# Reordering the start of a conv / attention / mixture-of-experts trunk, and moving its output bias to GpSimd

## The chip, the cores and the metric

The kernel runs on one core of one Trainium2 chip. The metric is the device time of one execution in microseconds; the kernel before takes 1702.82 us (median of 3 runs, 1698.28 to 1706.78). The core has five engines with instruction queues of their own: TensorE (PE; its weight loads are listed as PEld), VectorE (DVE), ScalarE (ACT), GpSimd (POOL) and SyncE (SP), which issues most transfers. The engines meet at semaphores. The transfers themselves run on 16 DMA engines of the core.

## The reference

Two residual layers over 512 tokens of width 1024, float32. Layer 0 mixes tokens with a Conformer convolution module, layer 1 with differential attention. After each comes a mixture of 32 gated experts, two for each token. The part that the change touches is the first mixer:

```python
def conformer_conv(h, w_in, b_in, dw, dw_b, ln_g, ln_b, w_out, b_out):
    u = h @ w_in + b_in                      # 1024 -> 2048
    a, g = jnp.split(u, 2, axis=-1)
    u = a * jax.nn.sigmoid(g)
    u = causal_depthwise_conv(u, dw) + dw_b  # 31 taps, each channel by itself
    u = jax.nn.silu(layer_norm(u, ln_g, ln_b))
    return u @ w_out + b_out
...
h = rms_norm(x, norm1_g[0])
x = x + conformer_conv(h, ...)               # this is where b_out comes in
h = rms_norm(x, norm2_g[0])
x = x + hierarchical_moe(h, ...)
```

## The kernel before, in words

All five engines run a hand-written program; nothing reorders it. Tokens lie in 4 tiles of 128, channels in 8 blocks of 128 (`ct`).

**Transfers.** SP issues them in program order (from L401): the four tiles of x (512 KB each, into `x_res`) with one small gain vector, then weight units 0 and 1 of `conv_w_in`, then the parameters of the convolution, then units 2 and 3, two units of `conv_w_out`, and 24 small ones. A weight unit is 2 MB, issued as two halves of 1 MB by `load_unit` (L315) into one of the six slots of `ring`. The parameters are six transfers that count on one semaphore, `params_loaded`: `conv_dw`, 31 rows of 4 KB (L408), three single rows of 4 KB (L410), the two rows of `conv_b_in` (L411), and the row of `conv_b_out` (L412). They go to `area3`, one parameter row per partition.

**Start.** For each token tile ACT takes the squares (L618), DVE inverts the root (L814), ACT scales the tile into `xn` (L624, semaphore `xn_done`), PE transposes it (L1158) and DVE writes it to `hT` (L820). PE then waits for all six parameter transfers, transposes the parameter rows in 8 small transposes into PSUM bank 5 (L1179), and DVE copies the result to `chan`, one column per parameter (L835), and signals `chan_taken` (L836). PE waits for that and for units 0 and 1, and begins the products.

**Products and convolution.** For each block `ct`, PE computes the two halves of the gated unit with 8 matmuls of 128x512 each (`project`, L1170) and signals `glu_ready`. ACT makes the gate (`gate`, L639), DVE the product (`gated`, L843, which needs `chan`). The 31 taps of a block are split: ACT multiplies 12 of them (L652) and POOL adds these up (L515), DVE does the other 19 (L860, L863), and then adds POOL's sum (L871, L872). Halfway through the taps of block ct, ACT makes the gate of block ct + 1, and stops there until PE has it. From ct = 3 on PE also sums the columns of finished blocks for the layer norm (`stats`, L1185, L1186), into banks 4 and 5.

**Output of the mixer.** `mix_out` (L1206) forms 8 results of 128 tokens by 512 columns. Each is 8 matmuls (L1221) and then one matmul of a row of ones with a half of the bias row (L1224), which adds `b_out`. DVE adds each result to `x_res` (`add_mix`, L892). In the second half PE puts the transposes of the next norm and the router's logits (L1158, L1240) between the results. Routing, the gather of rows by POOL (L525), and the expert loop follow (L1263 to L1290), each step released by the one before.

Of the kernel before, what the change touches and what calls it, by code (L numbers as in the profile page):

```python
# [27 lines left out]
ALU = mybir.AluOpType  # L28
# [3 lines left out]
P = 128  # L32
D = 1024
T = 512
NT = T // P
NC = D // P
EPS = 1e-6
TAPS = 31
# [27 lines left out]
def trunk(nc, x, norm1_g, norm2_g, conv_w_in, conv_b_in, conv_dw, conv_dw_b, conv_ln_g, conv_ln_b,  # L66
# [5 lines left out]
    def sb(name, shape, dt=F32):  # L72
        return ctx.enter_context(nc.sbuf_tensor(name, shape, dt))

    def sem(name):
        return ctx.enter_context(nc.semaphore(name))

    with ctx:

        x_res = sb("x_res", [P, NT, D])  # L80
# [3 lines left out]
        area2 = sb("area2", [P, UNIT])  # L84
        area3 = sb("area3", [P, UNIT])
        scratch = sb("scratch", [P, 5632])
        ident = sb("ident", [P, P])
        ones = sb("ones", [P, P])
# [29 lines left out]
        bank = [banks2[i // 2][:, i % 2, :] for i in range(8)]  # L118
# [10 lines left out]
        consts_ready, params_loaded, x_loaded = sem("consts_ready"), sem("params_loaded"), [sem(f"x_loaded{t}") for t in range(NT)]  # L129
# [6 lines left out]
        ssq_done, std_done, xn_done = sem("ssq_done"), sem("std_done"), sem("xn_done")  # L136
# [4 lines left out]
        chan_ready, chan_taken = sem("chan_ready"), sem("chan_taken")  # L141
        glu_ready, gate_done, u_done = sem("glu_ready"), sem("gate_done"), sem("u_done")
        tap_made, tap_added, conv_done, sq_done = sem("tap_made"), sem("tap_added"), sem("conv_done"), sem("sq_done")
        stats_ready, ln_var, ln_std, ln_x, ln_done = sem("stats_ready"), sem("ln_var"), sem("ln_std"), sem("ln_x"), sem("ln_done")
        mix_ready, mix_taken = sem("mix_ready"), sem("mix_taken")

        xn_stored, logits_ready, exp_in, exp_done = sem("xn_stored"), sem("logits_ready"), sem("exp_in"), sem("exp_done")
# [42 lines left out]
        def cols_dram(w, c0, width=512):  # L190

            v = w[:, c0:c0 + width].rearrange("(h p j) n -> h p j n", h=2, j=4)
            return [v[h] for h in range(2)]
# [12 lines left out]
        sq_ct = area1[:].rearrange("p (c t) -> p c t", c=NC)  # L206
        uT = area2[:].rearrange("p (c t) -> p c t", c=NC)
        chan_rows = area3[0:TAPS + 5, 0:D]
        b_out = area3[0:1, 3072:3072 + D]
        PAD = TAPS - 1  # L210
        u_buf = [scratch[:, b * (T + PAD):(b + 1) * (T + PAD)] for b in range(2)]
        base = 2 * (T + PAD)
# [52 lines left out]
        oT = area2[:].rearrange("p (h t) -> p h t", h=HEADS)  # L265
# [45 lines left out]
        def _(sp):  # L311
# [11 lines left out]
            def mix_unit(n, src):  # L323

                load_unit(chunk_halves(unit(n)), src, unit_loaded[n % RING])
# [74 lines left out]
            w_in, w_out = conv_w_in[0], conv_w_out[0]  # L400
            for t in range(NT):  # L401
                sp.dma_start(x_res[:, t, :], x[0, t * P:(t + 1) * P, :]).then_inc(x_loaded[t], 16)
                if t == 0:
                    sp.dma_start(norm_g[:, 0, :], norm1_g[0].rearrange("(h p j) -> p h j", h=2, j=4)).then_inc(gain_loaded, 16)
            mix_unit(0, cols_dram(w_in, 0))
            mix_unit(1, cols_dram(w_in, D))

            sp.dma_start(chan_rows[0:TAPS, :], conv_dw[0]).then_inc(params_loaded, 16)  # L408
            for r, vec in enumerate((conv_dw_b, conv_ln_g, conv_ln_b)):
                sp.dma_start(chan_rows[TAPS + r:TAPS + r + 1, :], vec).then_inc(params_loaded, 16)  # L410
            sp.dma_start(chan_rows[TAPS + 3:TAPS + 5, :], conv_b_in[0].rearrange("(r n) -> r n", r=2)).then_inc(params_loaded, 16)  # L411
            sp.dma_start(b_out, conv_b_out).then_inc(params_loaded, 16)  # L412
            mix_unit(2, cols_dram(w_in, 512))
            mix_unit(3, cols_dram(w_in, D + 512))
            for n in range(2):
# [18 lines left out]
            n0 = FIRST[1]  # L434
# [35 lines left out]
        def _(pool):  # L470
            g = nc.gpsimd
# [32 lines left out]
                                 pattern=[[1, P]], channel_multiplier=-1))  # L504
            g.memset(step_count[:], 0.0).then_inc(consts_ready, 1)


            k = 0
            for ct in range(NC):
# [292 lines left out]
        def _(dve):  # L802
# [44 lines left out]
            for ct in range(NC):  # L847
                ub = u_buf[ct % 2]
                dve.wait_ge(u_done, ct + 1)

                k0 = tap_count[0]
                for k, w in enumerate(range(POOL_TAPS, TAPS)):
                    acc = sums[k % 2]
                    dst = uT[:, ct, :] if w == TAPS - 1 else acc
                    if k >= 2:
                        dve.wait_ge(dve_taps, k0 + k - 1)
                    elif ct >= 1:
                        dve.wait_ge(conv_done, ct)
                    if k < 2:
                        ins = v.tensor_scalar(acc, ub[:, w:w + T], chan[:, ct, w:w + 1],  # L860
                                              chan[:, ct, TAPS:TAPS + 1] if k == 0 else 0.0, ALU.mult, ALU.add)
                    else:
                        ins = v.scalar_tensor_tensor(dst, ub[:, w:w + T], chan[:, ct, w:w + 1], acc, ALU.mult, ALU.add)  # L863
                    ins.then_inc(dve_taps, 1)
                tap_count[0] += TAPS - POOL_TAPS
                if ct + 1 < NC:
                    gated(ct + 1)
                dve.wait_ge(dve_taps, tap_count[0])
                dve.wait_ge(tap_added, (ct + 1) * (POOL_TAPS - 1))
                last = sums[(TAPS - POOL_TAPS) % 2]  # L870
                link(v.tensor_tensor(last, pacc[ct % 2], last, ALU.add))  # L871
                v.tensor_tensor(uT[:, ct, :], uT[:, ct, :], last, ALU.add).then_inc(conv_done, 1)  # L872
# [10 lines left out]
                v.tensor_tensor(uT[:, ct, :], uT[:, ct, :], ln_r, ALU.mult).then_inc(ln_x, 1)  # L883

            def add_mix(l):

                for n in range(2):
                    for t in range(NT):
                        k = NT * n + t
                        dve.wait_ge(mix_ready, 8 * l + k + 1)  # L890
                        xs = x_res[:, t, n * 512:(n + 1) * 512]
                        ins = v.tensor_tensor(xs, xs, mix_bank(l, k)[:], ALU.add)  # L892
                        if n == 0:
                            ins.then_inc(mix_taken, 1)
                        else:
                            ins.then_inc(x_done, 1)
                            invert_rms(N_MOE[l], t)
                            if t >= 1:
                                take_hT(N_MOE[l], t - 1)
                take_hT(N_MOE[l], NT - 1)  # L900
# [108 lines left out]
            for l in range(LAYERS):  # L1009
                n = N_MOE[l]  # L1010
# [137 lines left out]
        def _(pe):  # L1148
            mm = nc.tensor.matmul
# [23 lines left out]
            pe.wait_ge(consts_ready, 1)  # L1173
            for t in range(NT):
                transpose_xn(N_PRE[0], t)
            pe.wait_ge(params_loaded, 16 * 6)
            R = TAPS + 5
            for ct in range(NC):
                last = nc.tensor.transpose(bank[5][:, ct * R:(ct + 1) * R], chan_rows[:, ct * P:(ct + 1) * P], ident[0:R, 0:R])  # L1179
            last.then_inc(chan_ready, 1)  # L1180


            def stats(ct):
                pe.wait_ge(sq_done, ct + 1)
                mm(bank[4][:], ones[:], uT[:, ct, :], start=ct == 0, stop=ct == NC - 1)  # L1185
                return mm(bank[5][:], ones[:], sq_ct[:, ct, :], start=ct == 0, stop=ct == NC - 1)  # L1186

            pe.wait_ge(xt_taken, 8)
            pe.wait_ge(chan_taken, 1)
            for ct in range(NC):  # L1190
                ua, ug = (0, 1) if ct < 4 else (2, 3)
                loaded(pe, ua)
                loaded(pe, ug)
                if ct >= 2:
                    pe.wait_ge(u_done, ct - 1)
                cols = slice((ct % 4) * P, (ct % 4 + 1) * P)
                project(bank[2 * (ct % 2)][:], w_chunks(ua), hT, cols)
                last = project(bank[2 * (ct % 2) + 1][:], w_chunks(ug), hT, cols)
                last.then_inc(glu_ready, 1)
                if ct >= 3:  # L1200
                    stats(ct - 3)
            stats(NC - 3)
            stats(NC - 2)
            stats(NC - 1).then_inc(stats_ready, 1)

            def mix_out(l, n0, src, bias):  # L1206


                for n in range(2):
                    loaded(pe, n0 + n)  # L1210
                for n in range(2):
                    for t in range(NT):
                        k = NT * n + t
                        dst = mix_bank(l, k)
                        if n == 1:
                            pe.wait_ge(mix_taken, NT * l + t + 1)
                        for c in range(NC - 1 if k < ahead[l] else 0, NC):
                            if k == 0:

                                pe.wait_ge((ln_done, oT_done)[l], c + 1)  # L1220
                            last = mm(dst[:], src[:, c, t * P:(t + 1) * P], w_chunks(n0 + n)[:, c, :],  # L1221
                                      start=c == 0, stop=c == NC - 1 and not bias)
                        if bias:
                            last = mm(dst[:], ones[0:1, :], b_out[:, n * 512:(n + 1) * 512], start=False, stop=True)  # L1224
                        last.then_inc(mix_ready, 1)
                        if n == 1 and t >= 1:
                            transpose_xn(N_MOE[l], t - 1)
                        if n == 1 and t >= 2:
                            logits(l, t - 2)
                transpose_xn(N_MOE[l], NT - 1)  # L1230
                logits(l, NT - 2)
                logits(l, NT - 1)
# [126 lines left out]
                        pe.wait_ge(over_w2[l], j * 32 + 32)  # L1359
                        down(o, 0, unit(n1 + 2), j + 1).then_inc(o["y_ready"], 1)  # L1360

            mix_out(0, 4, uT, True)
            route(0)
            pe.wait_ge(lists_done, 1)
            experts(0)
# [4 lines left out]
            n0 = FIRST[1]  # L1370
# [106 lines left out]
            for h, g, e in attention_steps():  # L1477
# [51 lines left out]
                    output_T(e)  # L1529
                if h is not None:  # L1530
                    v_half(h, 1)
            mix_out(1, n0 + 6, oT, False)
            route(1)
            pe.wait_ge(lists_done, 2)
            experts(1)
# [22 lines left out]
```

## Time and profile before

| | us |
|---|---|
| median of 3 runs (lowest to highest) | 1702.82 (1698.28 to 1706.78) |
| the profiled execution, whole | 1700.86 |
| its span | 1699.1 |
| PE busy | 1408.8 (83%) |
| DVE busy | 440.7 (26%) |
| ACT busy | 328.0 (19%) |
| POOL busy | 277.2 (16%) |

The span covers the instructions of the program; 1.8 us of the execution lie around it. A matmul on float32 appears as two MATMUL instructions. Of the chain that ended last, 49% of the span is PE and 33% DMA, the latter nearly all the weights of the experts. The part that the change touches lies in the first 270 us: start to 31.5 us, products and convolution to 187 us, layer norm to 205 us, output of the mixer to 269 us. The granted TensorE clock is told in shares of full speed, 2.4 GHz; 0.5 is its lower level, 1.2 GHz.

### The profile page before, as it was taken

How to read it: one execution, taken by the hardware profiler on the slowest of the kernel's cores; microseconds unless marked ns; L12 is line 12 of the kernel's file. 1: busy time of each engine (PE TensorE's matmuls, PEld its weight loads, DVE VectorE, ACT ScalarE, POOL GpSimd, SP SyncE). 2: the span in 40 equal slices, each digit the busy share in tenths (PEclk: the TensorE clock that was granted, in tenths of full speed). 3: DMA queues.
4: the chain of work that ended last, by engine and by line, in shares of the span. 5: the costliest groups of instructions: out<-in, count | busy, mean ns of one | idle time of the engine just before them, and what ended most of it. 6: DMA issues, size and time to landing. Idle time of an engine off the chain costs nothing.

```text
span 1699.1 us, 17050 instructions
## 1 busy us (share of the span) xinstructions
PE 1408.8 (83%) x6028; PEld 638.2 (38%) x6028; DVE 440.7 (26%) x858; ACT 328.0 (19%) x629; POOL 277.2 (16%) x381
## 2 busy tenths in 40 slices
PE   4996596898878788777599999996997888888784
PEld 2442144333223223232376676644332332233231
DVE  1699615111011111010333333325110110110112
ACT  2465311000000000000334434421010000000000
POOL 0688200211111111110000000000211111111110
PEclk9998697999999999898799999997998999999997
DMA  9122015789999999998600400315899999999994
GB/s 324 37 99 99 1 74 222 318 361 419 420 420 420 420 421 418 419 416 339 248 1 1 149 1 1 149 74 223 338 360 420 421 420 420 420 416 413 418 413 184
DMA packets 91249, 473.13 MB, mean 278 GB/s; under 512 B 19675, under 2 KB 19675, under 8 KB 40260
## 3 DMA queue, kind: packets, MB, share of 16 engines
q1 hardware_dynamic: 78500, 443.12, 64.3%
q0 software_dynamic: 10400, 16.82, 2.7%
q10 hardware_dynamic: 2304, 12.58, 1.9%
q8 instruction: 29, 0.48, 0.1%
q14 instruction: 16, 0.13, 0.0%
HBM read 466.43 MB, written 23.33 MB: 288 GB/s over the span
## 4 chain that ended last, share of the span: by engine, by line
PE 49%; DMA 33%; DVE 7%; POOL 4%; issue 3%; SPq 3%; ACT 1%; ACTq 0%; POOLq 0%; DVEq 0%
DMA ring<-in_moe_w 30%; PE banks L1273 19%; PE banks L1381 7%; PE banks L1221 5%; POOL scratch L515 4%; PE banks L1290 3%; PE banks L1414 3%; SPq L315 2%; PE banks L1170 2%; DVE banks L863 2%; PE banks L1473 1%; PE banks L1428 1%; PE banks L1455 1%; DMA area<-y_dram 1%; PE banks L1402 1%
## 5 line engine op out<-in xcount | busy, mean ns | idle before, releaser
L1273 PE MATMUL banks<-ring,scratch 128*64 128x512 f32 x1984 | 502.2, 657 | 143.8 <-DMA ring<-in_moe_w 131.3
L1273 PEld LDWEIGHTS banks<-ring,scratch 128*64 128x64 f32 x1984 | 157.9, 151 | 484.8 <-issue 484.8
L1006 DVE COPY scratch<-banks 128x256 f32<-128x256 f32 x65 | 27.6, 424 | 801.7 <-PE banks L1281 801.7
L1290 PE MATMUL banks<-ring,scratch 128*64 128x512 f32 x1008 | 231.8, 602 | 3.0 <-DVE scratch L1006 3.0
L680 ACT ACTIVATE scratch<-banks 64x512 f32<-64x512 f32 x65 | 38.2, 588 | 598.8 <-PE banks L1273 598.8
L533 POOL COPY at_out<-rows_out 128x1 int32 (+1 forms) x64 | 11.6, 181 | 705.2 <-ACT scratch L684 705.2
L515 POOL TENSOR_TENSOR scratch<-scratch 128x512 f32<-128x512 f32 x88 | 111.8, 1271 | 63.6 <-ACT scratch L652 51.6
L1381 PE MATMUL banks<-hT,ring 128*128 128x512 f32 x256 | 117.9, 604 | 0.8 <-DVE hT L820 0.8
L1170 PE MATMUL banks<-hT,ring 128*128 128x512 f32 x256 | 113.2, 603 | 0.7 <-issue 0.7
L1290 PEld LDWEIGHTS banks<-ring,scratch 128*64 128x64 f32 x1008 | 68.3, 137 | 118.7 <-issue 111.7
L1221 PE MATMUL banks<-ring,area 128*128 128x512 f32 x200 | 91.3, 609 | 10.6 <-ACT area L662 9.6
L684 ACT ACTIVATE scratch<-banks 128x512 f32<-128x512 f32 x65 | 38.8, 597 | 286.0 <-PE banks L1290 286.0
L863 DVE SCALAR_TENSOR_TENSOR banks<-scratch,chan,banks 128x512 f32<-128x512 f32 x128 | 85.0, 748 | 0.0
L525 POOL DMA_INDIRECT scratch<-xn_dram,at_in x64 | 67.1, 1048 | 56.2 <-POOL at_in L522 53.9
L652 ACT ACTIVATE scratch<-scratch,chan 128x512 f32<-128x512 f32 x96 | 66.7, 718 | 49.0 <-POOL scratch L515 35.2
L536 POOL DMA_INDIRECT y_dram<-scratch,at_out x64 | 65.6, 1025 | 56.5 <-POOL at_out L533 56.5
L543 POOL MEMSET scratch<- 128x512 f32 x4 | 2.1, 524 | 437.1 <-DVE x_res L892 437.0
L1170 PEld LDWEIGHTS banks<-hT,ring 128*128 128x128 f32 x256 | 49.5, 194 | 63.0 <-issue 63.0
L1381 PEld LDWEIGHTS banks<-hT,ring 128*128 128x128 f32 x256 | 46.2, 190 | 49.5 <-issue 46.9
L1414 PE MATMUL banks<-ring,hT 128*128 128x128 f32 x512 | 60.4, 276 | 0.0
L1221 PEld LDWEIGHTS banks<-ring,area 128*128 128x128 f32 x200 | 37.6, 194 | 60.7 <-issue 55.6
L1414 PEld LDWEIGHTS banks<-ring,hT 128*128 128x128 f32 x512 | 58.4, 192 | 0.0
(205 smaller groups left out, 1144.6 us busy)
## 6 DMA issues: line engine op xcount, KB each, us to landing
ring<-in_moe_w SPq DMA_DIRECT2D x374, 1024.0 KB, 16.9
area<-in_moe_w SPq DMA_DIRECT2D x12, 1024.0 KB, 10.2
ring<-in_attn_w_qkv SPq DMA_DIRECT2D x12, 1024.0 KB, 14.6
ring<-in_conv_w_in SPq DMA_DIRECT2D x8, 1024.0 KB, 14.4
area<-y_dram ACTq DMA_DIRECT2D x8, 1024.0 KB, 7.9
ring<-in_conv_w_out SPq DMA_DIRECT2D x4, 1024.0 KB, 12.5
xn_dram<-area ACTq DMA_DIRECT2D x8, 512.0 KB, 2.7
hT<-in_moe_w SPq DMA_DIRECT2D x4, 1024.0 KB, 7.6
```

What stands on the lines that cost most here:

```text
L515: g.tensor_tensor(pacc[ct % 2], pacc[ct % 2], tap[(k - 1) % TAP_BUFS], ALU.add).then_inc(tap_added, 1)
L525: g.indirect_dma_start(out=xe[s], out_offset=None, in_=xn_dram[l][:, :], in_offset=bass.IndirectOffsetOnAxis(ap=at_in[:, s:s + 1], axis=0) ...
L536: g.indirect_dma_start(out=y_dram[l][:, :], out_offset=bass.IndirectOffsetOnAxis(ap=at_out[:, s:s + 1], axis=0), in_=y_sb[s], in_offset=No ...
L652: a.activation(dst, u_buf[ct % 2][:, w:w + T], ACT.Copy, scale=chan[:, ct, w:w + 1]).then_inc(tap_made, 1)
L684: a.activation(y_sb[s], bank[6 + s][:], ACT.Copy).then_inc(sems["y_taken"], 1)
L863: ins = v.scalar_tensor_tensor(dst, ub[:, w:w + T], chan[:, ct, w:w + 1], acc, ALU.mult, ALU.add)
L1170: last = mm(dst, w[:, c, cols], src[:, c, :], start=start and c == 0, stop=stop and c == NC - 1)
L1221: last = mm(dst[:], src[:, c, t * P:(t + 1) * P], w_chunks(n0 + n)[:, c, :], start=c == 0, stop=c == NC - 1 and not bias)
L1273: last = mm(bank[2 + s][q * SLOTS:(q + 1) * SLOTS, :], xeT[s][:, j, h, :], w[:, c, :], start=c == 0, stop=c == NC - 1)
L1290: last = mm(bank[6 + s][q * SLOTS:(q + 1) * SLOTS, :], hidT[s][:, j, :], w2c[:, j, q * 512:(q + 1) * 512], start=j == 0, stop=j == 3)
L1381: last = mm(qk_bank[c][:], w_chunks(u)[:, k, (h % 4) * P:(h % 4 + 1) * P], hT[:, k, :], start=k == 0, stop=k == NC - 1)
L1414: last = mm(v_bank[:, t * P:(t + 1) * P], hT[:, k, t * P:(t + 1) * P], w_chunks(u)[:, k, (h % 4) * P:(h % 4 + 1) * P], start=k == 0, stop= ...
```

## The change

It does four things.

1. SP issues the parameter transfers right behind x and in front of units 0 and 1. `conv_b_out` is no longer a row among them: it is loaded as 128 equal rows into `b_wide`, in the first quarter of `area2`, 512 KB in all, with a semaphore of its own, `bias_loaded`. `params_loaded` now counts five transfers.
2. PE does the products of block 0 first and the 8 parameter transposes behind them (`columns`). Its wait for `chan_taken` moves from ahead of all products to ct = 3, ahead of the first `stats`, which writes the bank that the transposes used.
3. The 8 bias results of `mix_out` go.
4. POOL adds `b_wide` to `x_res` tile by tile once ACT has read the tile for `xn`, in 4 additions of 128x1024, behind its constants and ahead of the taps. DVE waits for `bias_added` at the last two taps of block 0 (`area2`, where `b_wide` lies, is where the finished block is written) and ahead of `add_mix(0)`.

```diff
@@ sp
-            mix_unit(0, cols_dram(w_in, 0))
-            mix_unit(1, cols_dram(w_in, D))
-
             sp.dma_start(chan_rows[0:TAPS, :], conv_dw[0]).then_inc(params_loaded, 16)
             for r, vec in enumerate((conv_dw_b, conv_ln_g, conv_ln_b)):
                 sp.dma_start(chan_rows[TAPS + r:TAPS + r + 1, :], vec).then_inc(params_loaded, 16)
             sp.dma_start(chan_rows[TAPS + 3:TAPS + 5, :], conv_b_in[0].rearrange("(r n) -> r n", r=2)).then_inc(params_loaded, 16)
-            sp.dma_start(b_out, conv_b_out).then_inc(params_loaded, 16)
+            sp.dma_start(b_wide, conv_b_out.to_broadcast([P, D])).then_inc(bias_loaded, 16)
+            mix_unit(0, cols_dram(w_in, 0))
+            mix_unit(1, cols_dram(w_in, D))
             mix_unit(2, cols_dram(w_in, 512))
@@ pool
+            pool.wait_ge(bias_loaded, 16)
+            for t in range(NT):
+                pool.wait_ge(xn_done, t + 1)
+                g.tensor_tensor(x_res[:, t, :], x_res[:, t, :], b_wide, ALU.add).then_inc(bias_added, 1)
@@ dve, in the taps of a block
+                    if ct == 0 and w >= TAPS - 2:
+                        dve.wait_ge(bias_added, NT)
@@ dve, add_mix
+                if l == 0:
+                    dve.wait_ge(bias_added, NT)
@@ pe
-            pe.wait_ge(params_loaded, 16 * 6)
-            R = TAPS + 5
-            for ct in range(NC):
-                last = nc.tensor.transpose(bank[5][:, ct * R:(ct + 1) * R], chan_rows[:, ct * P:(ct + 1) * P], ident[0:R, 0:R])
-            last.then_inc(chan_ready, 1)
...
+            def columns():
+                pe.wait_ge(params_loaded, 16 * 5)
+                ...
+                last.then_inc(chan_ready, 1)
...
-            pe.wait_ge(chan_taken, 1)
             for ct in range(NC):
...
                 last.then_inc(glu_ready, 1)
+                if ct == 0:
+                    columns()
+                if ct == 3:
+                    pe.wait_ge(chan_taken, 1)
                 if ct >= 3:
                     stats(ct - 3)
@@ mix_out
                             last = mm(dst[:], src[:, c, t * P:(t + 1) * P], w_chunks(n0 + n)[:, c, :],
-                                      start=c == 0, stop=c == NC - 1 and not bias)
-                        if bias:
-                            last = mm(dst[:], ones[0:1, :], b_out[:, n * 512:(n + 1) * 512], start=False, stop=True)
+                                      start=c == 0, stop=c == NC - 1)
```

On SP, behind the small gain vector: `ring<-in_conv_w_in` are halves of units 0 to 3, the `area` rows the parameters. First before, then changed:

```order
L402 DMA x_res<-in_x 128x1024 x3
L315 DMA ring<-in_conv_w_in 128x4x512 x4
L408 DMA area<-in_conv_dw 31x1024
L410 DMA area<-in_conv_dw_b 1x1024
L410 DMA area<-in_conv_ln_g 1x1024
L410 DMA area<-in_conv_ln_b 1x1024
L411 DMA area<-in_conv_b_in 2x1024
L412 DMA area<-in_conv_b_out 1x1024
L315 DMA ring<-in_conv_w_in 128x4x512 x4
```

```order
L403 DMA x_res<-in_x 128x1024 x3
L406 DMA area<-in_conv_dw 31x1024
L408 DMA area<-in_conv_dw_b 1x1024
L408 DMA area<-in_conv_ln_g 1x1024
L408 DMA area<-in_conv_ln_b 1x1024
L409 DMA area<-in_conv_b_in 2x1024
L410 DMA area<-in_conv_b_out 128x1024
L316 DMA ring<-in_conv_w_in 128x4x512 x8
```

The four halves of units 0 and 1 moved behind five parameter transfers and the 128-row bias.

On PE, from the transposes of x (`area1`) to the first `stats`: `area3` is where the parameter rows lie, `hT,ring` are products. First before, then changed:

```order
L1158 MATMUL banks6_7<-ident,area1 128x128 x32
L1179 MATMUL banks4_5<-ident,area3 128x36 x8
L1170 MATMUL banks0_1<-hT,ring 128x512 x16
L1170 MATMUL banks2_3<-hT,ring 128x512 x16
L1170 MATMUL banks0_1<-hT,ring 128x512 x16
L1170 MATMUL banks2_3<-hT,ring 128x512 x16
L1185 MATMUL banks4_5<-area2,ones 128x512
```

```order
L1167 MATMUL banks6_7<-ident,area1 128x128 x32
L1179 MATMUL banks0_1<-hT,ring 128x512 x16
L1195 MATMUL banks4_5<-ident,area3 128x36 x8
L1179 MATMUL banks2_3<-hT,ring 128x512 x16
L1179 MATMUL banks0_1<-hT,ring 128x512 x16
L1179 MATMUL banks2_3<-hT,ring 128x512 x16
L1188 MATMUL banks4_5<-area2,ones 128x512
```

The 8 transposes moved from ahead of block 0 to between blocks 0 and 1.

## Rows read from the trace of the kernel before

**Rows 1.** Chain of waits in order of time, 0 to 360: start us, us, what.
```profile
15.83 13.85 DMA area<-in_conv_b_out
29.72 1.06 PE banks L1179 x8
30.79 0.72 issue
31.51 30.12 PE banks L1170 x64
61.65 0.69 ACT scratch L639
...
85.84 0.71 DVE banks L871
...
206.60 1.05 PE banks L1224 x2
207.66 7.06 PE banks L1221 x16
...
268.67 0.70 DVE x_res L892
269.39 1.16 ACT scratch L618 x2
...
300.17 2.79 DMA scratch<-xn_dram,at_in
```
**Rows 2.** Timeline, 18 to 53: start us, us, what [idle before <-releaser].
```profile
18.55 1.98 PE L1158 MATMUL banks<-ident,area 128*128 128x128 f32 x8 [0.76 <-DVE hT L820]
20.57 0.69 DVE L820 TENSOR_TENSOR hT<-banks,norm_g 128x512 f32<-128x512 f32 x1 [0.16 <-PE banks L1158]
30.83 0.46 DVE L835 COPY chan<-banks 128x288 f32<-128x288 f32 x1 [9.57 <-PE banks L1179]
...
52.18 8.35 POOL L515 TENSOR_TENSOR scratch<-scratch 128x512 f32<-128x512 f32 x6 [46.19 <-ACT scratch L652]
```
**Rows 3.** L315, second half of unit 1 alone: ns min/median/max, first and last start.
```profile
L315 SPq DMA_DIRECT2D ring<-in_conv_w_in x1: 642/642/642, 6.3 to 6.3; - x1
DMA to landing us min/median/max: 14.9/14.9/14.9
```
**Rows 4.** Stretches of the start: us, busy by engine, clock, DMA share, GB/s.
```profile
10.00:21.00 11.00, 7.90 (x32) 6.33 (x32) 5.29 (x11) 7.71 (x13) 0.00 (x0) 1.00 1.05 392
21.00:29.00 8.00, 0.00 (x0) 0.00 (x0) 0.26 (x1) 0.00 (x0) 0.00 (x0) 1.00 0.97 323
```
**Rows 5.** PE's matmuls of L1170, 31.4 to 36.4, then 36.4 to 47.9: ns min/median/max.
```profile
L1170 PE MATMUL banks<-hT,ring x6: 814/1061/1193, 31.5 to 35.9; 128*128 128x512 f32 x6
...
L1170 PE MATMUL banks<-hT,ring x28: 592/592/814, 35.9 to 47.7; 128*128 128x512 f32 x28
```
**Rows 6.** Waits, 0 to 360: us in total, times, longest us.
```profile
DVE x_res L892 <- PE banks L1224: 50.2, 8, 7.7
DVE banks L871 <- POOL scratch L515: 14.3, 8, 6.0
ACT scratch L639 <- PE banks L1170: 5.2, 2, 4.6
```
**Rows 7.** Groups of L1224 (PE, 200 to 272) and of L515 (the page).
```profile
L1224 PE MATMUL banks<-area,ones 1*128 1x512 f32 x16 | 9.0, 640 | 0.0
L515 POOL TENSOR_TENSOR scratch<-scratch 128x512 f32<-128x512 f32 x88 | 111.8, 1271 | 63.6 <-ACT scratch L652 51.6
```
**Rows 8.** Stretches from the output of the mixer to the first experts, as Rows 4.
```profile
230.00:277.00 47.00, 46.54 (x177) 25.24 (x175) 8.93 (x17) 12.93 (x18) 1.05 (x2) 1.00 0.36 135
277.00:300.00 23.00, 6.81 (x37) 3.45 (x36) 16.24 (x59) 0.42 (x2) 1.59 (x3) 0.63 0.65 274
```
**Rows 9.** Chain of waits, one later group of PE's transposes.
```profile
248.23 1.16 PE banks L1158 x8
```
**Rows 10.** L402, the four tiles of x (issued 0.8 to 2.7).
```profile
DMA to landing us min/median/max: 3.4/6.3/7.5
```

More of the change, by code:

```diff
@@ L144, in trunk @@
         stats_ready, ln_var, ln_std, ln_x, ln_done = sem("stats_ready"), sem("ln_var"), sem("ln_std"), sem("ln_x"), sem("ln_done")
+        bias_loaded, bias_added = sem("bias_loaded"), sem("bias_added")
         mix_ready, mix_taken = sem("mix_ready"), sem("mix_taken")
@@ L208, in trunk @@
         chan_rows = area3[0:TAPS + 5, 0:D]
-        b_out = area3[0:1, 3072:3072 + D]
+        b_wide = area2[:, 0:D]
         PAD = TAPS - 1
@@ L1186, in stats @@
                 return mm(bank[5][:], ones[:], sq_ct[:, ct, :], start=ct == 0, stop=ct == NC - 1)
+            def columns():
+                pe.wait_ge(params_loaded, 16 * 5)
+                R = TAPS + 5
+                for ct in range(NC):
+                    last = nc.tensor.transpose(bank[5][:, ct * R:(ct + 1) * R], chan_rows[:, ct * P:(ct + 1) * P], ident[0:R, 0:R])
+                last.then_inc(chan_ready, 1)
             pe.wait_ge(xt_taken, 8)
-            pe.wait_ge(chan_taken, 1)
             for ct in range(NC):
@@ L1204, in _, with mix_out @@
             stats(NC - 1).then_inc(stats_ready, 1)
-            def mix_out(l, n0, src, bias):
+            def mix_out(l, n0, src):
                 for n in range(2):
@@ L1360, in experts @@
                         down(o, 0, unit(n1 + 2), j + 1).then_inc(o["y_ready"], 1)
-            mix_out(0, 4, uT, True)
+            mix_out(0, 4, uT)
             route(0)
@@ L1531, in _ @@
                     v_half(h, 1)
-            mix_out(1, n0 + 6, oT, False)
+            mix_out(1, n0 + 6, oT)
             route(1)
```

## The prediction, made before the changed kernel ran

> **What bounds the kernel now.** I read the chain of waits first, because the page's busy shares are means over stages with different limits. Up to the first product the chain is a transfer: the last parameter row is issued at 15.83 us and is the thing waited for until 29.72; then come PE's 8 small transposes (1.06), the copy to `chan` and a signal (0.72), and the products from 31.51 [rows 1]. The timeline shows that everything else is ready earlier: the last half of `hT` is written at 20.57 + 0.69 = 21.26 [rows 2], and unit 1 has landed at 6.3 + 14.9 = 21.2 [rows 3]. So 31.51 - 21.26 = 10.2 us of PE lie idle or on parameters. Then the chain runs through 30.12 us of products (blocks 0 and 1) to the gate of block 1 at 61.65, which ACT had been waiting for during 4.6 us [rows 1, 6], and from there through POOL's taps to DVE at 85.84 [rows 1]. DVE waited 6.0 us for POOL at the end of block 0 [rows 6], so in the first blocks it is the second gate that counts, and not the first. The output of the mixer, to 268.67, is PE back to back: 46.54 of the 47 us from 230 to 277 are busy [rows 8], and each of its 8 results ends with a bias product on the chain, 1.05 us for its two instructions [rows 1].
>
> Behind that all is released by what came before. The first expert's chain goes through the gather of rows at 300.17 [rows 1], not through weights. What is won before 300 us is therefore passed on whole; the expert loop keeps its own length.
>
> **The bias products.** 8 results, one matmul each (16 instructions in the group [rows 7]), 1.05 us from row to row of the chain: 8 x 1.05 = 8.4 us go. What was hidden behind them must still fit. In the second half the next norm of a tile is one DVE addition (0.70), the squares on ACT (1.16 with the root's start [rows 1]), an inversion and a second pass of ACT over the same tile, some 4 us, and it has the next result's 7.06 us of products [rows 1] to hide in. DVE's 50.2 us of waiting for the last product of each result [rows 6] say that it has room. So I take all 8.4.
>
> **GpSimd's additions.** POOL does 128x512 in 1.27 us [rows 7], so 128x1024 is about 2.5 and four are 10.2 us. They need the bias and `xn`. If the bias lands at 20 us, they are done at 30; POOL's own taps begin at 52.18 [rows 2] and DVE's new wait stands at the end of block 0, near 62 us. Cost nothing, cover 20 us or more. Were the bias over 20 us late, this cost would count one for one.
>
> **The start, where I had to choose.** The change pays only if units 0 and 1 still land early with the parameters in front. By bytes, the parameters are 31 + 3 + 2 rows of 4 KB = 147 KB, which is 0.4 us at 392 GB/s, and the wide bias is 524 KB, 1.3 us [rows 4]. By these, unit 1 lands at 21.2 + 1.7 = 22.9. But this is not how the parameters moved before. The last one took 13.85 us from issue to landing [rows 1]. The unit in front landed at 21.2, and only 8.5 us later were the parameters there, at 29.68. Meanwhile the core still moved 323 GB/s of units behind them, against 392 ahead [rows 4]. So they did not wait for the core's bandwidth, but went one behind another on a narrow part of it, 37 rows in 8.5 us, or 0.23 us for a row, and they stayed in order with the unit ahead of them. If that part also carries a share of each unit, units 0 and 1 now end where the parameters ended. Everything that stood ahead of 29.68 still stands ahead of it, only in another order, with the bias now 128 rows instead of one.
>
> A rule bears on this. The Trainium skill (DMA: Bandwidth & Descriptors, "Why a DMA increments its semaphore by 16 and not by 1") says that a transfer is spread over k engines, k being the largest number up to 16 that divides the outer count of rows. For 31 rows, k is 1, and on one engine the parts of all transfers stand in a queue. By that rule the transfers of 31 rows and of one row all go to the first engine, which also owes a sixteenth of every unit; a unit counts as landed only when that engine is done. The 8.5 us for 37 rows agree. By the opposite reading, that small transfers cost their bytes, the forecast would be the first rival below.
>
> Order kept: unit 1 lands at 29.68 + 1.3 (bias) - 0.2 (the one row that it replaces) = 30.8. This is the upper end for a bias that spreads like x. The lower end is 22.9. In between, the rows might be faster with no other units beside them; at half their 0.23 us unit 1 would land at 26.5. I take 30.8, the value nearest to what the parameters did. The first product then starts at 30.8 instead of 31.51: -0.7 us.
>
> Then what moves behind it. The 8 transposes now stand between blocks 0 and 1. They took 1.06 us at 29.72, at the lower clock: the 8 small transposes of x took 1.98 at 18.55 and 1.16 at 248 [rows 2, 9], so warm they are 1.06 x 1.16 / 1.98 = 0.6. +0.6 us. The clock itself: PE had to start cold and still will. The first instructions of L1170 took 1061 ns in the median and then 592 [rows 5]; by their starts, 31.5 to 36.4 ran at half speed. The windows grant 1.00 there, but the durations are those of 1.2 and then 2.4 GHz. Before, 1.06 us of transposes preceded the products; now PE comes out of 10 us of idleness straight into them. A cold stretch that ends by 1.8 us later costs half of that, 0.9; one that ends as before costs nothing. I take 0.4. The gate of block 0 is later by the two terms just named, the copy to `chan` (0.46 [rows 2]) and a signal, about 1.7 us less the 0.7; the 4.6 us in which ACT waited for block 1 hide it, since block 1 itself comes 0.3 later.
>
> Sum at the gate of block 1: -0.7 + 0.6 + 0.4 = +0.3. With the output, -8.4 + 0.3 = -8.1 us against the profiled execution: span 1699.1 - 8.1 = 1691.0, whole 1692.8. The median lies 2.0 us above that execution, so 1694.7.
>
> The bounds of the start term run from -8.6 + 0.6 + 0 = -8.0 (unit 1 at 22.9) to +1.5 or so (rows as slow as before, cold stretch at its longest, the wide bias at 0.23 us a row for its 8 rows on that part). The forecast's own range, with 2.5 us for the scatter of a median of runs that spread over 8.5, is 1689 to 1699.
>
> **Rivals.**
>
> *The parameters cost their bytes.* Then the first product starts at 22.9 to 23, 8.5 us earlier, and with +0.6 and +0.4 the start gives -7.5. Total -15.9: 1687. For it: small amounts of data, and the transfers that follow (24 tiny ones). Against it: 8.5 us for 147 KB. Chance 0.13.
>
> *The gain is taken back before the experts.* The output gets 8.4 us shorter, but something that doesn't move with PE ends last there, most plausibly the weights for the first experts (fetched from the release of ring slots in this stage), or the clock, which stood at 0.63 between 277 and 300 [rows 8]. 1701 to 1703. Against it: DMA runs at 0.36 of its share from 230 to 277 and the gather is what the first expert waits for. Chance 0.06.
>
> *The wide bias goes down the narrow part.* It is 128 rows. If its source, which is one row read 128 times, puts all of them on the path of the parameters, it takes 128 x 0.23 = 29 us, unit 1 lands at 59 and the first product starts 27.9 us later. POOL's additions and DVE's new wait move with it. Total -8.4 + 27.9 + 1 = +20: 1723. It decides from the point where the bias takes over 8 us there. Against it: each tile of x is 128 rows of 4 KB too, and all four had landed by 2.7 + 7.5 = 10.2 us [rows 10]. Chance 0.03.
>
> **Chances.** Forecast 0.78, rivals 0.13, 0.06 and 0.03. What a measurement of this kernel can tell from no change is about 0.5%, 8.5 us, and the forecast lies just inside of it at 8.1. Of its 0.78 I put 0.38 beyond the bound, as the open bounds of the start point more to the early side. Faster: 0.38 + 0.13 = 0.51. Within: 0.40 + 0.06 = 0.46. Slower: 0.03. The range must hold most of the first rival's side and the second's: 1686 to 1700.
>
> **What the changed profile would show.** The chain's first long piece is a weight unit of `conv_w_in`, ending near 30.8; at 23 the first rival is right, at 59 the third. Between blocks 0 and 1 stand 8 small transposes of about 0.6 us in all. The gate of block 1 begins near 62.0. POOL's four additions of about 2.5 us lie between 20 and 31, and no DVE wait names them. From the first L892 to the last, the output is 8.4 us shorter, and the gather stands at about 292. I am wrong if the start gives more than 3 us, or if the shift at the gather is not that of the gate of block 1 plus 8.4.

## The result, and the profile after

The changed kernel takes 1691.86 us (median of 6 runs, 1686.43 to 1695.07) against 1701.88 for the kernel before (6 runs). The ratio is 0.9933, 95% interval 0.9917 to 0.9950, that is 8.5 to 14.1 us less. Two more sets of six runs, told below, gave 0.9949 (0.9932 to 0.9966) and 0.9942 (0.9926 to 0.9959). The three together say some 10 us less, where 8.1 were forecast; all three medians lie between 1691 and 1694. Two executions of the kernel before in a later set (1783.71 and 7731.79 us) were in a slow state, and the ratios leave them out. The profiled execution is among the slower ones: 1694.97 us, span 1693.1, only 6.0 under the span before.

The chain of waits of the changed kernel, in order of time (start us, us, what), answers to [rows 1]:

```profile
8.55 20.22 DMA ring<-in_conv_w_in
28.91 16.09 PE banks L1179 x32
45.00 0.62 PE banks L1195 x8
45.62 13.94 PE banks L1179 x32
59.59 0.69 ACT scratch L644
...
201.44 35.46 PE banks L1234 x82
236.90 0.95 PE banks L1167 x8
237.85 6.87 PE banks L1234 x16
...
247.72 7.08 PE banks L1234 x16
...
254.82 0.70 DVE x_res L901
...
290.75 2.78 DMA scratch<-xn_dram,at_in
```

The first long piece is now a weight unit, and it ends at 28.8, neither at 22.9 nor at 59. The 8 transposes stand between blocks 0 and 1 and take 0.62 us. The gate of block 1 begins at 59.59 instead of 61.65. The mixer's output is one run of products, and a result takes 6.87 us where it took 7.06 + 1.05 = 8.11 [rows 1]. Its last addition begins 268.67 - 254.82 = 13.85 us earlier. But the gather ends only 9.4 us earlier, and the span 6.0: what was won in the first 255 us is partly lost behind. The 13.85 us are 2.1 at the gate of block 1, 0.6 in the blocks behind it, 1.4 in the last column sums and 9.8 from there on, in the output. The 1.4 us are no merit of the change. The last column sums ahead of the layer norm, the same two pairs of instructions in both kernels, ran at the lower clock before and at the higher one after; in the chain of before, then of after:

```profile
183.66 2.08 PE banks L1185 x2
185.74 1.33 PE banks L1186 x2
```

```profile
181.02 1.13 PE banks L1188 x2
182.14 0.87 PE banks L1189 x2
```

GpSimd's timeline (start us, us, instruction, and the idle time before it with its releaser):

```profile
18.42 9.25 POOL L511 TENSOR_TENSOR x_res<-x_res,area 128x1024 f32<-128x1024 f32 x4 [12.41 <-DMA area<-in_conv_b_out]
49.29 8.35 POOL L520 TENSOR_TENSOR scratch<-scratch 128x512 f32<-128x512 f32 x6 [21.62 <-ACT scratch L657]
```

The four additions start when the wide bias lands, at 18.4, take 2.3 us each, and leave 21.6 us of idleness. In the list of waits of the first 360 us (total, times, longest) DVE has no line for POOL's additions, `bias_added`; three lines of it:

```profile
DVE x_res L901 <- PE banks L1234: 40.4, 8, 6.5
DVE banks L878 <- POOL scratch L520: 14.5, 8, 6.8
ACT scratch L644 <- PE banks L1179: 6.0, 2, 5.4
```

DVE still waits for PE at each result, for 40.4 us instead of 50.2 [rows 6]: the difference of 9.8 us is, within the rounding, what the output got shorter.

Where does the part behind 255 us go? The stretches that answer to [rows 8] (us, busy by engine, granted clock, DMA share, GB/s):

```profile
230.00:277.00 47.00, 38.27 (x167) 26.11 (x165) 15.46 (x45) 13.35 (x20) 1.05 (x2) 0.80 0.50 197
277.00:300.00 23.00, 13.99 (x38) 5.73 (x40) 10.53 (x33) 0.00 (x0) 5.04 (x8) 0.59 0.40 152
```

Two stretches hold other work than before, since all has moved. Still, within them stand the last transposes and the last logits, the same work in each kernel, and they show the clock: in the timeline of this execution,

```profile
258.45 1.98 PE L1167 MATMUL banks<-ident,area 128*128 128x128 f32 x8 [0.67 <-DVE hT L825]
260.23 3.47 PE L1251 MATMUL banks<-w_route,hT 128*128 128x36 f32 x16
```

and in a second profiled execution of the same program (`changed_again`, below):

```profile
260.52 1.23 PE L1167 MATMUL banks<-ident,area 128*128 128x128 f32 x8 [0.67 <-DVE hT L825]
261.58 1.87 PE L1251 MATMUL banks<-w_route,hT 128*128 128x36 f32 x16
```

1.98 against 1.23 and 3.47 against 1.87: the first execution does them at 1.2 GHz and the second at 2.4. What PE did right before was the same in both: a run of products, the transposes and logits of the tile before, and a pause of 0.67 us. From the mixer's last addition to the issue of the gather the kernel before takes 29.2 us, this execution 33.6 and the second one 29.2. The chain accounts for the difference: 0.75 us in these transposes, 1.55 and 1.65 in the two groups of 16 logits, 0.46 in the small products behind them. So the loss in front of the gather is the clock, and not the change's own cost.

Behind the gather the same can be read at two groups of equal work, the 64 matmul instructions of the first expert and the first 24 of the attention layer; in the chain of before, then of after:

```profile
304.13 14.82 PE banks L1273 x64
832.59 10.57 PE banks L1381 x24
```

```profile
294.71 16.24 PE banks L1284 x64
825.13 12.21 PE banks L1392 x24
```

The granted clock of the first 5 us of each group is 0.81 and 1.00 before, 0.53 and 0.66 after. These two groups hold 3.1 of the 3.4 us that the changed kernel takes longer from the issue of the gather to the end of the span. What makes the clock fall there is not shown.

### The profile page after: what moved, and what is told of

Same layout as the page of the kernel before. It is cut to its first block, busy times and chain, and to the rows that moved or that the text cites. A ratio compares the mean times of both kernels' runs of the same rounds, so it can differ in the third digit from the quotient of the medians.

```text
span 1693.1 us, 17025 instructions
## 1 busy us (share of the span) xinstructions
PE 1411.0 (83%) x6012; PEld 643.0 (38%) x6012; DVE 441.0 (26%) x858; ACT 328.2 (19%) x629; POOL 287.1 (17%) x385
## 4 chain that ended last, share of the span: by engine, by line
PE 49%; DMA 33%; DVE 7%; POOL 4%; issue 3%; SPq 2%; ACT 1%; ACTq 0%; POOLq 0%; DVEq 0%
DMA ring<-in_moe_w 31%; PE banks L1284 19%; PE banks L1392 7%; PE banks L1234 5%; POOL scratch L520 4%; PE banks L1301 4%; PE banks L1425 3%; SPq L316 2%; PE banks L1179 2%; DVE banks L870 2%; PE banks L1484 1%; PE banks L1439 1%; DMA ring<-in_conv_w_in 1%; PE banks L1466 1%; DMA area<-y_dram 1%
## 5 line engine op out<-in xcount | busy, mean ns | idle before, releaser
L1234 PE MATMUL banks<-ring,area 128*128 128x512 f32 x200 | 90.1, 608 | 10.5 <-ACT area L667 9.4
L1392 PEld LDWEIGHTS banks<-hT,ring 128*128 128x128 f32 x256 | 46.8, 192 | 50.5 <-issue 47.9
L1425 PE MATMUL banks<-ring,hT 128*128 128x128 f32 x512 | 60.4, 276 | 0.0
```

The lines of the kernel that those rows point to most:

```text
L1392: last = mm(qk_bank[c][:], w_chunks(u)[:, k, (h % 4) * P:(h % 4 + 1) * P], hT[:, k, :], start=k == 0, stop=k == NC - 1)
L1425: last = mm(v_bank[:, t * P:(t + 1) * P], hT[:, k, t * P:(t + 1) * P], w_chunks(u)[:, k, (h % 4) * P:(h % 4 + 1) * P], start=k == 0, stop= ...
```

## The experiments

All are compared with the kernel before, run in the same rounds. The table has the marks of each profiled execution, in us. "Output" is the start of DVE's last addition of the mixer; "whole" is the ratio of the runs with its interval.

| kernel | first product | gate of block 1 | output | gather issued | span | whole |
|---|---|---|---|---|---|---|
| before | 31.51 | 61.65 | 268.67 | 297.88 | 1699.1 | 1 |
| changed | 28.91 | 59.59 | 254.82 | 288.46 | 1693.1 | 0.9933 (0.9917 to 0.9950) |
| changed_again | 28.61 | 60.13 | 256.89 | 286.08 | 1690.9 | 0.9949 (0.9932 to 0.9966) |
| changed_third | 28.88 | 59.37 | 254.47 | 288.10 | 1692.6 | 0.9942 (0.9926 to 0.9959) |
| start_only | 28.80 | 60.42 | 269.29 | 302.26 | 1704.6 | 0.9985 (0.9972 to 0.9999) |
| bias_only | 30.91 | 60.49 | 257.06 | 288.58 | 1690.3 | 0.9932 (0.9915 to 0.9949) |
| bias_only_second | 30.61 | 60.33 | 257.03 | 288.57 | 1688.1 | 0.9949 (0.9931 to 0.9968) |
| split_taps | 24.19 | 55.07 | 250.21 | 283.72 | 1687.7 | 0.9910 (0.9894 to 0.9927) |
| split_bias_late | 22.60 | 53.44 | 248.60 | 282.14 | 1686.9 | 0.9897 (0.9875 to 0.9920) |
| split_columns_first | 22.55 | 52.85 | 249.85 | 279.06 | 1678.2 | 0.9904 (0.9883 to 0.9925) |
| before_split | 24.59 | 54.62 | 263.51 | 296.50 | 1699.2 | 0.9971 (0.9958 to 0.9983) |
| bias_full_rows | 30.23 | 59.57 | 262.30 | 291.53 | | |
| bias_twice | 30.30 | 60.59 | 277.82 | 307.06 | | |

**start_only.** The parameters in front and the transposes behind block 0, on the kernel before; the bias stays a row and the bias products stay.

```diff
-            mix_unit(0, cols_dram(w_in, 0))
-            mix_unit(1, cols_dram(w_in, D))
             sp.dma_start(chan_rows[0:TAPS, :], conv_dw[0]).then_inc(params_loaded, 16)
...
             sp.dma_start(b_out, conv_b_out).then_inc(params_loaded, 16)
+            mix_unit(0, cols_dram(w_in, 0))
+            mix_unit(1, cols_dram(w_in, D))
```

> The start of the change alone: parameter transfers (the bias still one row among them) in front of units 0 and 1, transposes behind block 0; the bias products stay. Theory (rows on one narrow path, units queue behind them): the wide bias no longer stands ahead, so the first product starts 1.1 us earlier than the 28.9 of the changed kernel, near 27.8, the gate of block 1 near 58.5 (before 61.65), whole kernel -3.1 us. Rival (the gain of the changed kernel is mostly its start, and the bias products were cheap): whole kernel -8 us or more. Rival (the start gives nothing that lasts): 0.

The first product came at 28.80, not at 27.8: leaving out the wide bias brought nothing here. The gate of block 1 moved by 1.2 us, not 3.1, because block 0 took 17.03 us in this execution, with a longer stretch at the low clock, where the changed kernel's took 16.09. At the end of the mixer nothing was left of it in this execution (269.29 against 268.67), since its last result took 9.59 us instead of 7.06, told at the end. Over the runs the start alone is worth 0.0015, 2.6 us, from 0.2 to 4.8: small, as the first theory has it.

**bias_only.** The changed kernel with the start undone.

```diff
+            mix_unit(0, cols_dram(w_in, 0))
+            mix_unit(1, cols_dram(w_in, D))
             sp.dma_start(chan_rows[0:TAPS, :], conv_dw[0]).then_inc(params_loaded, 16)
...
             pe.wait_ge(xt_taken, 8)
+            columns()
+            pe.wait_ge(chan_taken, 1)
             for ct in range(NC):
```

> The bias part alone: GpSimd adds the wide bias, no bias products, but the parameters (and the wide bias behind them) stay behind units 0 and 1 and the transposes ahead of block 0. Theory (a bias product costs 1.24 us, not 1.05, since the period of a result fell from 8.11 to 6.87 us in the changed kernel): first product near 31.3 as before, period of a result 6.87, whole kernel -9.9 us. Rival (8.4 us as predicted, the rest of the gain from the start): period 7.06, whole kernel -8.4. GpSimd's four additions end before 40 us and nobody waits for them.

The chain of its output:

```profile
203.68 35.46 PE banks L1233 x82
239.14 0.95 PE banks L1168 x8
240.10 6.87 PE banks L1233 x16
```

6.87 us for a result, and 11.6 us for the whole (8.7 to 14.5). This part alone gives as much as the whole change. The rival's period of 7.06 is refuted. GpSimd's four additions run from 30.12 to 39.37, and DVE has no wait for them.

**bias_full_rows and bias_twice.** What a bias product costs. In the first, the one-row matmul is replaced by one of 128 rows; in the second it is issued twice. Both change the output and with it the routing behind, so they are read up to the gather.

```diff
-                            last = mm(dst[:], ones[0:1, :], b_out[:, n * 512:(n + 1) * 512], start=False, stop=True)
+                            last = mm(dst[:], ones[:], w_chunks(n0 + n)[:, 0, :], start=False, stop=True)
```

> The kernel before, with each bias product replaced by a matmul of 128 rows (ones, 128x128, by 128x512 of the weights; the mixer's output is therefore not the reference's). Before, a result took 8.11 us of which 6.87 are its 8 products when they stand alone. Theory (the one-row form costs 0.38 us more than its 0.86 because the stream changes shape): a result takes 9 x 0.859 = 7.73 us, mixer's output 3 us shorter than before. Rival (any ninth product costs 1.24, for instance since it ends the group): 8.11.

> The kernel before with every bias product issued twice in a row (the bias is added twice, so the mixer's output is not the reference's; read up to the gather only). Before, a result takes 8.11 us, 1.24 of it for one bias product. Theory (the extra 0.38 us are for the change between 128-row and 1-row matmuls and back, once a group): the second product costs 0.86 us and a result takes 8.97. Rival (each one-row matmul costs 1.24): 9.35.

The chain of bias_full_rows, then of bias_twice:

```profile
204.03 6.87 PE banks L1221 x16
210.90 0.86 PE banks L1224 x2
211.76 6.87 PE banks L1221 x16
```

```profile
207.54 7.06 PE banks L1221 x16
214.60 1.05 PE banks L1224 x2
215.65 0.86 PE banks L1225 x2
216.51 7.07 PE banks L1221 x16
```

6.87 + 0.86 = 7.73, and 7.06 + 1.05 + 0.86 = 8.97, both as the theory said. A ninth product of full rows costs 0.86. The one-row form costs 0.19 more on itself and 0.19 more on the 128-row matmuls next to it, once for a change of shape and not for each instruction. Two more rows agree: the 8 transposes behind a bias product took 1.16 us [rows 9] and take 0.95 without it, and the one result of the changed kernel that still stands behind a one-row product, that of the router's bias, takes 7.08. The chain had shown the first of these 0.19 in the row of the bias, and the second in the row of the products, 7.06 where 6.87 is the bare length.

**split_taps.** The changed kernel, with the 31 rows of `conv_dw` issued in two pieces.

```diff
-            sp.dma_start(chan_rows[0:TAPS, :], conv_dw[0]).then_inc(params_loaded, 16)
+            for r0, r1 in ((0, 16), (16, TAPS)):
+                sp.dma_start(chan_rows[r0:r1, :], conv_dw[0, r0:r1, :]).then_inc(params_loaded, 16)
```

> The changed kernel, with the 31 rows of conv_dw issued as two transfers of 16 and 15 rows. Theory (31 rows go down one engine's queue since 31 has no divisor up to 16 but 1; 16 and 15 rows spread over 16 and 15 engines): 29 rows of about 0.22 us leave the queue ahead of the units, the first product starts 5.5 to 6.4 us earlier, near 22.9 (from 28.9), the gate of block 1 near 53.5, whole kernel 6 us under the changed kernel. Rival (the units are late because SP issues eight halves behind more transfers, or because of bytes): first product within 0.5 us of 28.9, no change in the whole.

```profile
24.19 16.30 PE banks L1180 x32
40.48 0.61 PE banks L1196 x8
41.10 13.95 PE banks L1180 x32
```

The same bytes to the same places, and the first product comes 4.4 to 4.7 us earlier than in the changed kernel. The whole is at 0.9910, its median 5.8 us under that of the changed kernel in the same rounds (1688.12 against 1693.91), and the intervals of the two ratios don't touch. The rival said no change and is refuted; the size at the first product was 1 us less than expected.

**before_split.** The same edit, alone, on the kernel before.

> The kernel before with one edit: the 31 rows of conv_dw as two transfers of 16 and 15 rows, still behind units 0 and 1; bias products kept. Theory (the queue of one engine, not the place of the transfers, made the wait): the parameters land 6 to 7 us earlier, near 23, the first product starts near 25 instead of 31.5, whole kernel -6.5 us. That is more than reordering gave (-2.7 us at the first product). Rival (transfers of the parameters are late because they stand behind 4 MB of units): first product 31.5 within 0.5.

```profile
13.61 9.14 DMA area<-in_conv_b_out
22.79 1.07 PE banks L1180 x8
24.59 30.01 PE banks L1171 x64
```

The parameters, still behind the 4 MB of units 0 and 1, are there at 22.75 instead of 29.68, and the first product starts at 24.59. Against 31.51 that is 6.9 us, and against the 30.2 to 30.9 of four other executions with the old start some 6; reordering had brought about 2. So the place in the order was hardly the matter, the 31 rows were. The records of the single DMA packets in the traces show it directly. In the kernel before, the 37 packets of 4 KB that are the parameters follow one another without overlap for 8.5 us, 0.16 to 0.33 us each; in before_split most of them overlap, and all lie within 3.0 us.

The whole gained 4.9 us (2.9 to 7.1), less than the 6.5 expected. The profile shows one place where gain is lost: the gate of block 1 is 7.0 us earlier and the last addition only 5.2, and the last result in front of it took 9.61 us where it takes 7.06 in the kernel before.

**split_bias_late and split_columns_first.** Two steps on from split_taps: the wide bias behind units 0 and 1, and then the transposes ahead of block 0 again.

```diff
-            sp.dma_start(b_wide, conv_b_out.to_broadcast([P, D])).then_inc(bias_loaded, 16)
             mix_unit(0, cols_dram(w_in, 0))
             mix_unit(1, cols_dram(w_in, D))
+            sp.dma_start(b_wide, conv_b_out.to_broadcast([P, D])).then_inc(bias_loaded, 16)
...
+            columns()
             pe.wait_ge(xt_taken, 8)
+            pe.wait_ge(chan_taken, 1)
             for ct in range(NC):
```

> split_taps, with the wide bias (524 KB) issued behind units 0 and 1 instead of ahead of them. Theory (the first engine's queue now decides by its length, and 8 rows of 0.16 us leave it): first product 1.3 us earlier than the 24.2 of split_taps, near 22.9; whole kernel 1 us under split_taps, about -16 against before. GpSimd's additions start near 24 and still end before 40, nobody waits. Rival (start_only, which had no wide bias ahead of the units, started no earlier than the changed kernel: the wide bias fills gaps and costs nothing): first product 24.2 again.

> split_bias_late, with the 8 parameter transposes ahead of block 0 again, as in the kernel before: since the parameters now land near 12 us, PE can do them while it waits for unit 1. Theory (the transposes behind block 0 cost 0.6 us on the path and are only useful when the parameters are late): first product as in split_bias_late, the gate of block 1 0.6 us earlier than there, whole kernel the same within its interval. Rival (the wait for chan_taken ahead of the products costs its 0.7 us again): gate of block 1 no earlier.

The late bias gives 1.6 us at the first product (22.60 from 24.19), so the wide bias does cost time once the 31 rows no longer hold the units up, about the 1.3 us that the prediction had worked out from its bytes. The last half of unit 1 was also issued 1.6 us earlier, at 7.69 instead of 9.26, so the bytes and the place in the order are not told apart. The whole is 17.5 us under before, where about 16 were expected. With the transposes first, PE does them at 20.46 while it waits, in its timeline:

```profile
20.46 1.06 PE L1196 MATMUL banks<-ident,area 36*128 36x36 f32 x8
22.55 41.85 PE L1180 MATMUL banks<-hT,ring 128*128 128x512 f32 x91 [1.03 <-DMA ring<-in_conv_w_in]
```

The gate of block 1 is another 0.59 us earlier, as expected. The two versions are the fastest here, at 0.9897 and 0.9904, and their intervals don't tell them apart. The interval of split_bias_late ends at 0.9920; those of the changed kernel's three sets, from other rounds, begin at 0.9917, 0.9932 and 0.9926. So it is the faster one by two of the three, and the third overlaps by 0.0003; between the middles lie 6 to 9 us.

**changed_again, changed_third, bias_only_second.** The same programs once more.

> The changed kernel once more, unaltered. Theory (the profiled execution lost some 4 us of its gain behind the mixer's output to the TensorE clock, which is a matter of the single execution): the first product starts at 28.9 within 0.3 and the period of a result is 6.87 again, but the start of the gather, 288.5 in the first profile, differs by up to 4 us, and the median of the runs stays 10 to 12 us under before. Rival (the loss belongs to the change): the gather starts at 288.5 within 0.5 again.

> The changed kernel unaltered, on the same chip and in the same rounds as bias_only_second. Theory (its start gives 1 to 2 us at the mixer and the TensorE clock blurs that later): median 0 to 3 us under bias_only_second, 8 to 12 under before; first product at 28.6 to 28.9, period of a result 6.87. Rival (the new order of the start costs something): median above bias_only_second by more than 1.5 us once more.

> The bias part alone, unaltered from bias_only, to hold against the changed kernel in the same rounds. Theory: first product near 30.9, period of a result 6.87, whole kernel 9 to 11.5 us under before, 0 to 3 us above the changed kernel.

The gather was issued at 288.46, 286.08 and 288.10 us in three executions of one program, while the first product differed by 0.3. That part of the loss belongs to the single execution: from the last addition to the gather they take 33.6, 29.2 and 33.6 us. Another part came back each time: from the gather to the end of the span all three lose 3.3 to 3.6 us against before, and the two executions of bias_only lose 0.5 and gain 1.7. The first expert's 64 instructions took 16.24, 16.39 and 16.21 us in the three, 15.24 and 15.22 in bias_only and 14.82 before; the 24 of the attention layer 12.21, 12.37 and 12.16, against 10.57 in the three others. No edit touches anything there. So it is the clock again, but why it falls in the one program and not in the other stays open.

The median of changed_again is 9.8 us under before, where 10 to 12 were expected. Changed and bias_only are equal in the last rounds (1693.56 and 1693.57), and 2.2 us apart in the earlier ones with the changed kernel behind. So whether the new start brings anything once the bias products are gone stays open. Its gate of block 1 comes at 59.7 us in the mean of three executions, that of bias_only at 60.4 in the mean of two: these 0.7 us are less than what the clock does behind.

## Why the prediction was right, and where it was off

- *The start is bound by transfers, not by `hT`*, and the parameters hold up the units wherever they stand. Right, and shown: splitting one transfer moved the first product by 4.4 us and more in the new order, and by some 6 in the old. The rule of the Trainium skill (DMA: Bandwidth & Descriptors, "Why a DMA increments its semaphore by 16 and not by 1") was the right one against bytes: 31 rows on one engine, 16 and 15 rows on many. The first rival (22.9) was wrong in the changed kernel; the first product came near its time once the rows were split, at 24.2, and at 22.6 with the bias behind the units.
- *Unit 1 at 30.8.* Mis-sized: it was 28.8. The sum had put 8.5 us of rows, 1.1 of bias and 11 of units behind x. The bias had landed at 18.4, so rows and bias took 8.2 us from the 10.2 of x [rows 10], and the units 10.4. Besides, 31.51 was a late start: other executions with the old start have 30.2 to 30.9. The start term was -2.6 in the profiles and about -2 over several, not -0.7.
- *Transposes +0.6.* Measured 0.62.
- *Cold clock +0.4.* About right. The products of blocks 0 and 1 took 29.3 to 30.3 us in the seven executions with the transposes in front of them, mean 29.9, and 29.8 to 31.0 in the six without, mean 30.4 and so 0.5 more. Between two single executions it can have either sign: block 0 took 16.45 us before and 16.09, 16.93 and 15.90 in the changed kernel's three.
- *Gate of block 1 at +0.3.* It was -2.06, -1.52 and -2.28 against the one profile of before. But that profile is a late one: the five executions with the old order and the 31 rows in one piece have the gate at 59.6 to 61.7, mean 60.5, and the four with the new order at 59.4 to 60.4, mean 59.9. So the new start is worth 0.6 to 0.7 us at this point: -1.9 at the first product, +0.6 for the transposes, +0.6 for the cold clock. That the gate of block 0 is later than the first product's gain and costs nothing was right: ACT still waited 5.4 us for block 1.
- *8.4 us for the bias products.* The mis-sized term of this part: 8 x 1.24 = 9.9, and 9.8 in the profile from the column sums to the last addition. I had read the price from the row of the bias alone, while the products' row next to it held another 0.19 us each, and [rows 1] showed only 7.06 without a bare result to compare it with.
- *GpSimd's additions cost nothing.* Right: 18.4 to 27.7, cover 21.6 us.
- *All of it is passed on.* Over the runs this holds about as far as they can tell: -0.7 and -9.8 make -10.5 us at the end of the mixer, and the medians give some 10. In the profiled execution it was wrong: of 13.85 us, 9.4 arrive at the gather and 6.0 at the end. By the prediction's own sign of being wrong, the shift at the gather should have been that of the gate plus 8.4, which is 10.5; it was 9.4. The output gave 1.4 more than 8.4, the blocks and the column sums in front of it another 2.0, and the clock took 4.4 back. The second rival named both candidates. Weights for the first experts play no part, since the gather still ends last there. The clock is shown, by equal work at two levels: 1.98 against 1.23 us and 3.47 against 1.87 ahead of the gather, 16.24 against 14.82 and 12.21 against 10.57 behind it.
- *The wide bias on the narrow part* did not happen: it was there at 18.4.

The forecast, 1694.7, is above the measured medians by 1 to 3 us. The mechanisms of both parts were right. Both direct terms were too small, the bias by 1.4 to 1.5 us and the start by about 1, taken over several executions. Of these 2.4 us the runs show some 2, -10 where -8.1 was forecast. The rest of the distance lies in the starting point, a median of 1702.82 over three runs that became 1701.88 over six.

## What to carry to other kernels

A transfer like these 31 rows is priced by the length of one queue and not by bytes (37 packets one after another, 8.5 us for 152 KB), and the large transfers behind it waited for that queue; look for the last small transfer's time from issue to landing, and split it before reordering anything. An instruction of another shape in a run of equal ones is priced by the period of the run with it and without it, not by its own row (1.24 us against 1.05 here). A gain of under 1% must be read at marks near the edit, over several executions, because the clock's steps behind it were as large here: 4.4 us ahead of the gather, some 3 behind it.

## What was not expected of the hardware

- 31 rows of 4 KB in one transfer held the 4 MB behind them up by 4.4 us more than as 16 and 15 rows, which are the same bytes.
- One change between 128-row and 1-row matmuls and back costs 0.38 us beside the 0.86 of the matmul itself.
- The same program does the same transposes behind the same pause at 1.2 GHz in one execution (1.98 us) and at 2.4 in another (1.23), and so takes 33.6 us in one and 29.2 in the other from the mixer's last addition to the gather.
- In start_only the clock fell within a run of products: one result that takes 7.06 elsewhere took 9.59.

```profile
255.82 2.23 PE banks L1244 x16
258.05 0.57 PE banks L1245 x2
258.61 9.59 PE banks L1225 x16
```

In front of it PE had done one group of transposes and 16 small matmuls of logits, between two full results. The same result took 9.61 us in before_split and 9.21 in bias_twice, and 7.06 or 7.08 behind the same work in all the other executions. The marks of start_only, before_split and bias_twice at the output and the gather carry these 2.1 to 2.6 us.
